# Spreading a factor by one-pass products and adding six tiles to a stored residual by accumulating DMAs

## The reference, cut to what matters

```python
def rmsnorm(x, g):
    y = x * lax.rsqrt(jnp.mean(x * x, axis=-1, keepdims=True) + EPS)
    return y * g

x = x + rmsnorm(merged @ w_o, g_post_mix)
f = jnp.square(jax.nn.relu(rmsnorm(x, g_pre_ffn) @ w1)) @ w2
x = x + rmsnorm(f, g_post_ffn)          # the end: f, its norm per token, the residual
```

## Time and profile before

| | |
|---|---|
| Median of 3 runs | 1711.32 us (1710.51, 1711.32, 1711.40) |
| The profiled execution | 1711.26 us, span 1709.5 us |
| Granted TensorE clock, mean | 0.997 |
| Busy share of the span | TensorE 99%, VectorE 77%, ScalarE 51%, GpSimd 6% |
| From HBM, to HBM | 221.20 MB, 60.69 MB |

### The profile page before, as it was taken

The page is one execution under the profiler, slowest core; times in us unless marked ns, Lnnn a source line. Parts: engine busy times, 40 slices in busy tenths (PEclk is TensorE's granted clock), DMA queues, the critical chain, the costliest instruction groups (busy, mean ns, idle before and its releaser), DMA issues.

```text
span 1709.5 us, 31894 instructions
## 1 busy us (share of the span) xinstructions
PE 1698.6 (99%) x12687; PEld 1685.4 (99%) x12687; DVE 1324.2 (77%) x2538; ACT 868.9 (51%) x1681; POOL 106.2 (6%) x143
## 2 busy tenths in 40 slices
PE   9999999999999999999999999999999999999997
PEld 9999999999999999999999999999999999999997
DVE  7778877878788777668688788777878887777665
ACT  7636454555554545446366374545545536444452
POOL 1311211000000000000002221000000000000000
PEclk9999999999999999999999999999999999999998
DMA  7889989454321322233138898444623313322231
GB/s 249 219 199 215 252 222 241 125 175 155 112 74 51 112 87 87 87 99 99 62 121 221 209 232 217 133 140 114 201 106 99 99 54 98 97 88 87 74 99 56
DMA packets 94133, 233.64 MB, mean 137 GB/s; under 512 B 9888, under 2 KB 21408, under 8 KB 93984
## 3 DMA queue, kind: packets, MB, share of 16 engines
q1 hardware_dynamic: 72352, 179.16, 32.9%
q0 software_dynamic: 20352, 50.34, 14.6%
q10 hardware_dynamic: 1280, 2.10, 0.3%
HBM read 221.20 MB, written 60.69 MB: 165 GB/s over the span
## 4 chain that ended last, share of the span: by engine, by line
PE 99%; DVE 1%; ACT 0%; issue 0%; DVEq 0%
PE ring L820 20%; PE ring L822 20%; PE ring L821 20%; PE att L820 12%; PE att L822 11%; PE att L821 11%; PE att L3680 1%; PE att L815 1%; PE att L814 1%; PE att L827 0%; PE ring L3516 0%; PE att L3496 0%; PE att L828 0%; PE att L3843 0%; ACT rope_s L1289 0%; PE att L3503 0%
## 5 line engine op out<-in xcount | busy, mean ns | idle before, releaser
L820 PE MATMUL ring<-xs_hi,w_lo 128*128 128x288 f32 x1792 | 532.8, 297 | 0.6 <-issue 0.4
L822 PE MATMUL ring<-xs_hi,w_hi 128*128 128x288 f32 x1792 | 527.9, 295 | 0.0
L821 PE MATMUL ring<-xs_lo,w_hi 128*128 128x288 f32 x1792 | 527.7, 294 | 0.0
L2133 DVE TENSOR_TENSOR w_lo<-w_raw,w_hi 128x1024 fp32r<-128x1024 f32 (+1 forms) x370 | 377.1, 1038 | 27.7 <-ACT w_hi L1218 19.0
L820 PEld LDWEIGHTS ring<-xs_hi,w_lo 128*128 128x128 f32 x1792 | 336.6, 188 | 2.9 <-issue 1.2
L821 PEld LDWEIGHTS ring<-xs_lo,w_hi 128*128 128x128 f32 x1792 | 336.8, 188 | 1.3
L822 PEld LDWEIGHTS ring<-xs_hi,w_hi 128*128 128x128 f32 x1792 | 336.6, 188 | 0.0
L822 PE MATMUL att<-f_hi,w_hi 128*128 128x288 f32 x960 | 283.2, 295 | 0.0
L821 PE MATMUL att<-f_lo,w_hi 128*128 128x288 f32 x960 | 282.9, 295 | 0.0
L820 PE MATMUL att<-f_hi,w_lo 128*128 128x288 f32 x960 | 282.6, 294 | 0.0
L820 PEld LDWEIGHTS att<-f_hi,w_lo 128*128 128x128 f32 x960 | 180.4, 188 | 0.0
(11 more groups left out here) (355 smaller groups left out, 3215.5 us busy)
## 6 DMA issues: line engine op xcount, KB each, us to landing
w_raw<-blocks_in SPq DMA_DIRECT2D x189, 512.0 KB, 3.7
weight_sums<-blocks_in POOLq DMA_DIRECT2D x72, 512.0 KB, 7.0
w_raw<-weight_sums SPq DMA_DIRECT2D x96, 256.0 KB, 4.4
w_raw<-blocks_in SPq DMA_DIRECT2D x70, 256.0 KB, 4.2
weight_sums<-weight_sums POOLq DMA_DIRECT2D x48, 256.0 KB, 6.7
small_raw<-small_in SPq DMA_DIRECT2D x16, 320.0 KB, 5.0
small_raw<-small_in SPq DMA_DIRECT2D x32, 128.0 KB, 5.2
my_kept<-rx SPq DMA_DIRECT2D x12, 288.0 KB, 6.1
```

Source lines behind the costliest of these rows:

```text
L820: pe.matmul(out, w[1], x[0], start=first, stop=False)
L821: pe.matmul(out, w[0], x[1], start=False, stop=False)
L822: return pe.matmul(out, w[0], x[0], start=False, stop=last)
L2133: return dve.tensor_tensor(out, a, hi.bitcast(F32), ALU.subtract)
```

## The change

The spread factor is no longer made by three fp32 products but by six fp32r products, from a rounded part `last_hi` and its rest `last_lo`, which VectorE makes after the reciprocal; ScalarE makes a rounded copy of the identity in `last_ident`, ahead of the first `last_scaled`. The tail's pieces are now tiles 0 and 1, 2 and 3, 4 and 5 (`TAIL_SUMMED`) and 6 and 7 (`TAIL_ADDED`). SP stores tiles 0 to 5 of the second half of `x` as they are before the feed-forward result is added, behind its last weight load; GpSimd's queue, once this store has landed, adds each factored piece of `last` straight from SBUF to the stored values in memory. VectorE adds tiles 6 and 7 as before, and ScalarE's queue stores them. SP's last wait is for both kinds.

```diff
-TAIL_MOVED, TAIL_ADDED = [(0, 1), (1, 3), (3, 4)], [(4, 6), (6, 8)]
+TAIL_SUMMED, TAIL_ADDED = [(0, 2), (2, 4), (4, 6)], [(6, 8)]
+SUMMED = TAIL_SUMMED[-1][1]
...
+        sp.wait_ge(pl.x_new, x_new(DEPTH - 1, "wo_b", KC - 1))
+        sp.dma_start(x_out[:, 0:SUMMED, cols(1)], pl.x[:, 0:SUMMED, cols(1)]).then_inc(pl.tail_stored, 16)
         sp.wait_ge(pl.x_new, x_new(DEPTH - 1, "post_a", KC - 1))
         sp.dma_start(x_out[:, :, cols(0)], pl.x[:, :, cols(0)]).then_inc(pl.x_stored, 16)
-        for i, (m0, m1) in enumerate(TAIL_MOVED):
-            sp.wait_ge(pl.tail_moved, i + 1)
-            sp.dma_start(x_out[:, m0:m1, cols(1)], pl.x[:, m0:m1, cols(1)]).then_inc(pl.x_stored, 16)
-        sp.wait_ge(pl.x_stored, 16 * (1 + len(TAIL_MOVED) + len(TAIL_ADDED)))
+        sp.wait_ge(pl.x_stored, 16 * (1 + len(TAIL_ADDED)))
+        sp.wait_ge(pl.tail_summed, 16 * len(TAIL_SUMMED))
...
-        for i, (m0, m1) in enumerate(TAIL_MOVED):
+        pool.wait_ge(pl.tail_stored, 16)
+        for i, (m0, m1) in enumerate(TAIL_SUMMED):
             pool.wait_ge(pl.tail_factored, i + 1)
-            nc.gpsimd.tensor_tensor(pl.x[:, m0:m1, cols(1)], pl.x[:, m0:m1, cols(1)], pl.last[:, m0:m1, :], ALU.add) \
-                .then_inc(pl.tail_moved, 1)
+            pool.dma_start(x_out[:, m0:m1, cols(1)], pl.last[:, m0:m1, :], accum_op=ALU.add).then_inc(pl.tail_summed, 16)
...
+                act.activation(pl.last_ident[0:TRI, 0:TRI], pl.const(C_ID, P)[0:TRI, 0:TRI], ACT.Copy) \
+                    .then_inc(pl.tail_scaled, 1)
                 last_scaled(0)
...
-        dve.reciprocal(pl.last_root[0:TRI, 0:3], pl.last_root[0:TRI, 0:3]).then_inc(pl.tail_spread, 1)
+        own.step(dve.reciprocal(pl.last_inv[0:TRI, 0:3], pl.last_root[0:TRI, 0:3]))
+        own.wait()
+        own.step(dve.tensor_copy(pl.last_hi[0:TRI, 0:3], pl.last_inv[0:TRI, 0:3]))
+        own.wait()
+        minus(pl.last_lo[0:TRI, 0:3], pl.last_inv[0:TRI, 0:3], pl.last_hi[0:TRI, 0:3]).then_inc(pl.tail_spread, 1)
         eng.wait_ge(pl.tail_full, 1)
-        eng.wait_ge(pl.tail_scaled, KC)
-        for m0, m1 in TAIL_MOVED + TAIL_ADDED:
+        eng.wait_ge(pl.tail_scaled, KC + 1)
+        for m0, m1 in TAIL_SUMMED + TAIL_ADDED:
...
         eng.wait_ge(pl.tail_spread, 1)
+        eng.wait_ge(pl.tail_scaled, 1)
         for i in range(3):
-            root_i = pl.last_root[0:TRI, i:i + 1].broadcast_to([TRI, P])
-            last = pe.matmul(att[:, LAST_R + TRI * i:LAST_R + TRI * (i + 1)], root_i, ident[0:TRI, 0:TRI],
-                             start=True, stop=True)
+            out = att[:, LAST_R + TRI * i:LAST_R + TRI * (i + 1)]
+            pe.matmul(out, pl.last_lo[0:TRI, i:i + 1].broadcast_to([TRI, P]), pl.last_ident[0:TRI, 0:TRI],
+                      start=True, stop=False)
+            last = pe.matmul(out, pl.last_hi[0:TRI, i:i + 1].broadcast_to([TRI, P]), pl.last_ident[0:TRI, 0:TRI],
+                             start=False, stop=True)
         last.then_inc(pl.tail_full, 1)
```

More of the change, by code:

```diff
@@ L494, in __init__ @@
         self.tail_added = semaphore("tail_added")
-        self.tail_moved = semaphore("tail_moved")
+        self.tail_stored = semaphore("tail_stored")
+        self.tail_summed = semaphore("tail_summed")
         self.ff_read = semaphore("ff_read")
@@ L575, in memory @@
         self.last_root = self.nc.alloc_sbuf_tensor_at("last_root", [P, 4], F32, offset=self.xh_at + 4 * KC * NH)
+        self.last_inv = self.nc.alloc_sbuf_tensor_at("last_inv", [P, 4], F32, offset=self.xh_at + 4 * KC * NH + 32)
+        self.last_hi = self.nc.alloc_sbuf_tensor_at("last_inv_hi", [P, 4], F32R,
+                                                    offset=self.xh_at + 4 * KC * NH + 64)
+        self.last_lo = self.nc.alloc_sbuf_tensor_at("last_inv_lo", [P, 4], F32R,
+                                                    offset=self.xh_at + 4 * KC * NH + 96)
+        self.last_ident = self.nc.alloc_sbuf_tensor_at("last_ident", [P, P], F32R,
+                                                       offset=self.xh_at + 4 * KC * NH + 128)
         small_at = mark[0]
@@ L855, in program @@
         loads(nc, block, pl, x_in, consts, tables, blocks, small, uv, cache_t, cache_n, cache_pe, x_out)
-        rotation_and_sums(nc, block, pl, blocks)
+        rotation_and_sums(nc, block, pl, blocks, x_out)
         scalar_engine(nc, block, pl, x_in, x_out, kv_out, kpe_out, conv_out)
@@ L1104, in _, with rotation_and_sums @@
             w2_load(7, 3)
+        sp.wait_ge(pl.x_new, x_new(DEPTH - 1, "wo_b", KC - 1))
+        sp.dma_start(x_out[:, 0:SUMMED, cols(1)], pl.x[:, 0:SUMMED, cols(1)]).then_inc(pl.tail_stored, 16)
         sp.wait_ge(pl.x_new, x_new(DEPTH - 1, "post_a", KC - 1))
         sp.dma_start(x_out[:, :, cols(0)], pl.x[:, :, cols(0)]).then_inc(pl.x_stored, 16)
-        for i, (m0, m1) in enumerate(TAIL_MOVED):
-            sp.wait_ge(pl.tail_moved, i + 1)
-            sp.dma_start(x_out[:, m0:m1, cols(1)], pl.x[:, m0:m1, cols(1)]).then_inc(pl.x_stored, 16)
-        sp.wait_ge(pl.x_stored, 16 * (1 + len(TAIL_MOVED) + len(TAIL_ADDED)))
-def rotation_and_sums(nc, block, pl, blocks):
+        sp.wait_ge(pl.x_stored, 16 * (1 + len(TAIL_ADDED)))
+        sp.wait_ge(pl.tail_summed, 16 * len(TAIL_SUMMED))
+def rotation_and_sums(nc, block, pl, blocks, x_out):
     @block.gpsimd
@@ L3451, in _ @@
         for i, (m0, m1) in enumerate(TAIL_ADDED):
-            eng.wait_ge(pl.tail_factored, len(TAIL_MOVED) + 1 + i)
+            eng.wait_ge(pl.tail_factored, len(TAIL_SUMMED) + 1 + i)
             dve.tensor_tensor(pl.x[:, m0:m1, cols(1)], pl.x[:, m0:m1, cols(1)], pl.last[:, m0:m1, :], ALU.add) \
```

## The result

| | time, us (median) | runs | lowest to highest |
|---|---|---|---|
| before, same chip | 1710.38 | 6 | 1709.68 to 1711.40 |
| changed kernel | 1720.32 | 6 | 1719.30 to 1721.29 |

The ratio is 1.0057, with a 95% interval of 1.0047 to 1.0068: 9.9 us slower, where 2.6 were forecast and the range ended at 1717.4. The profiled execution took 1719.3 us, with a span of 1717.5 against 1709.5.

The account below looks back on a forecast made before the run. TensorE bounds all but the tail, whose end passes from VectorE's last add to GpSimd's queue: last landing 1709.1 to 1711.7, span 1712.1, plus 1.76 gives 1713.9 us, 2.6 slower; range 1710.6 to 1717.4.

Parts of the forecast that it names:

- Step 1: VectorE after the reciprocal: a rounding copy and a subtraction, delaying TensorE's first load by 0.39 us.
- Step 2: TensorE's spread: six fp32r products at half clock take 1.57 us against 1.45; first multiply starts 0.52 later.
- lower bound: TensorE's spread takes 0.9 us if the clock holds at 1.00 throughout.
- Steps 3 to 6: Tail: identity copy and residual stores cost nothing; multiplies 0.67 apart; last add takes 0.74, its store lands at 1708.4.
- branch that was to gain 0.7: VectorE's add of tiles 6 and 7 and its store: add ends at 1705.98, against 1706.66 before.
- Step 7: Three GpSimd accumulates of tiles 0 to 5, issued 0.95 apart, paced by queue bytes; last landing at 1711.7 us.
- price of one alone: One 288 KB accumulate on GpSimd's queue, with no other, lands after 5.1 us.
- queue price: Each further 288 KB accumulate in GpSimd's queue costs 1.46 us, by bytes.
- half share of the plain store: Store of tiles 6 and 7 beside the accumulates: half of a share bounded by 0 and 0.8 us.
- first issue's lag: GpSimd's first accumulate can start 0.09 us after the multiply's end, at 1703.29.
- Accumulates paid by the run: Rival, chance 0.26: accumulates cost per run, not per byte, 2.6 us each behind one another; 1717.7 us, or 1721.
- Quick accumulates: Rival, chance 0.12: each accumulate lands within 3.2 us, the plain store lands last; 1710.6 us.

Follow-up runs that it names:

- acc_only: The changed kernel with the spread in fp32 products as before, keeping the residual store and three accumulating DMAs; 1719.71 us, ratio to before 1.0055.
- room_1088: The changed kernel with 1088 bytes of DMA descriptor room (dynamic_dma_scratch_size) in place of 1024; 1719.73 us, ratio to before 1.0054.
- one_run: The changed kernel with the output laid out half by half, so each accumulate has half the runs for the same bytes; 1714.39 us, ratio to before 1.0022.
- plain: The changed kernel with GpSimd's three accumulates turned into plain stores, leaving out the residual's addition in six tiles; 1711.12 us, ratio to before 1.0002.
- acc_two: The changed kernel with only tiles 0 and 1 accumulated by GpSimd, tiles 2 to 7 added by VectorE; 1713.06 us, ratio to before 1.0014.

## Why the prediction was wrong, point by point

**Step 1, VectorE's two more operations: right.** Reciprocal, copy and subtraction start at 1699.33, 1699.54 and 1699.74, and the first load 0.62 after the reciprocal's start, where before had 0.22: 0.40 more, 0.39 said.

**Step 2, the spread: wrong in its clock, 0.7 too dear.** I said that all six products would run at half clock and take 1.57. The six loads started 0.11 apart at full clock, and the first multiply followed 0.91 after the first load, the lower bound that I had given. The changed kernel's windows (us, busy time of PE, PEld, DVE, ACT, POOL, then the granted clock):

```profile
1699.90:1700.80 0.90, 0.85 (x6) 0.74 (x6) 0.00 (x0) 0.00 (x0) 0.00 (x0) 1.00 0.00 0
1700.80:1701.80 1.00, 0.02 (x1) 0.00 (x0) 0.94 (x2) 0.00 (x0) 0.00 (x0) 1.00 0.00 0
1701.80:1702.80 1.00, 0.00 (x0) 0.00 (x0) 1.00 (x2) 0.00 (x0) 0.42 (x1) 0.78 0.00 0
1702.80:1703.80 1.00, 0.00 (x0) 0.00 (x0) 0.97 (x3) 0.00 (x0) 0.82 (x1) 0.50 0.00 0
```

The fall from 2.4 to 1.2 GHz came between 1701.8 and 1702.8 (the mean of 0.78 puts it near 1702.4), 1.7 us later than in the earlier trace rows, and I had taken one execution's moment for a fixed one. From reciprocal to first multiply it is 1.53 where before had 1.70. But the split isn't what gained it: acc_only kept the fp32 products, found the same full clock, and took 1.17. At equal clock the split costs 0.35: 0.39 by VectorE's two operations (0.62 against 0.23 from reciprocal to first load), of which the products give back 0.04 (0.91 against 0.95 from first load to first multiply). In room_1088 the same six products ran at half clock, and reciprocal to first multiply took 2.17.

**Steps 3 to 6: right, but for one landing.** GpSimd's wait ahead of its first accumulate was ended by VectorE's multiply (the 628.96 us idle, above), not by the stored residual; the multiplies start 0.67 apart; the add takes 0.76 (0.74 said). Its store landed 3.5 after the issue where I took 2.3, beside the accumulates; it didn't matter, since it was off the path. The branch that was to gain 0.7 lands at T + 7.1, as before's.

**Step 7, the accumulates: this step failed.** "So issues stand at 1703.29, 1704.24, 1705.19": they began 1.5, 6.6 and 11.5 after T. The price of one alone was nearly right (4.7 for a stated 5.1), and so was its order behind the wait; what was wrong was that a second could be queued before the first had landed. Two issues in a row of before were my evidence; they were of 256 runs and 128, of 2 KB each, which fit together, and 256 with 256 doesn't. The queue price was mis-sized too, though the changed kernel never paid it: 1.46 for each further 288 KB, where the second landed 2.9 behind the first in room_1088, and the others 2.8 and 1.9 apart in one_run. The half share of the plain store, 0.4, doesn't show: the accumulate beside it took 4.8, the two alone 4.6 and 4.7. The first issue's lag was also mis-sized: 0.09 after the multiply's end was arithmetic's distance, and a DMA instruction on GpSimd began 0.77 after it (1702.38, the multiply's end being 1701.61), in before's L1128 0.58 after the landing it waited for.

Put together, from T: 0.75 for the multiply, 0.77 for the lag, then three landings of 4.7 and two turn-arounds of 0.35 make 16.3; 16.2 was measured. The forecast had 9.2 (1711.7 less 1702.46). These 7.0 us are the failure; the time missed by 6.4.

**The rivals.** "Accumulates paid by the run" foresaw the time (1717.7 to 1721; the upper figure leaves out the store's 0.8 that the lower one counts) and its sign. That is luck, since its mechanism, a queue interval of 2.6 to 4.7 on the DMA engines, isn't what the trace shows: the engines rest between the transfers. Runs matter after all, though by the room that they take and not by their time: in one_run half the runs moved the same bytes hardly faster (the second landed 2.8 after the first, in room_1088 with twice the runs 2.9), and yet the end came 5.5 us sooner. "Quick accumulates" has its answer in 4.7 for one alone.

## What to carry to other kernels

Read the waits of every queue to which a change hands work, above all those that end in nothing shown: here a GpSimd that idled on "issue" between DMAs was out of descriptor room, and each further transfer cost a full landing, not its bytes. More room isn't free either: the three kernels that had it reached T 2 to 7 us later than the changed kernel, in one profile each. Count runs before handing GpSimd accumulates, and lay the target out in long runs. A DMA that takes over an add at the end of a kernel is paid by its landing, which here was six times as long as the add.

## What the runs showed of the hardware

- GpSimd's DMAs in flight are limited by the descriptor room that the program reserves: 1024 bytes held three accumulates of 128 runs or one of 256, 1088 two of 256 or one of 256 with two of 128 (but only three of 128), 1152 four of 128; three plain stores of 256 runs fit into 1024. The next issue begins 0.26 to 0.36 after a landing. In the tail it was always the landing of the last one outstanding; in before L1140 was released by L1133's while L1137 was still on its way, 22 times out of 22. When room is given back is not settled.
- The Trainium skill, SBUF — State Buffer, section on SBUF's size, counts 16 KiB per partition for this scratch. This kernel reserves 1 KiB, and the measured limits move with that number.
- An accumulate from SBUF of 288 KB in 256 runs, with no other in flight, took 4.5 to 4.9 us from issue to landing, a plain store of the same shape from GpSimd 2.7 (the first of plain's), and from ScalarE 2.3.
- Beside accumulates a plain store of 288 KB landed after 3.5 (after), 3.8 (acc_two, median of three) and 7.1 us (one_run, behind three of them); beside three plain stores after 3.4 (plain).
- GpSimd begins a DMA instruction 0.6 to 0.8 us after what it waits for, an addition 0.09 after.
- The moment at which TensorE's clock falls in an idle tail differs between executions of like kernels: within the spread in before, plain and acc_two, 1.5 us behind its end in after, ahead of its start in room_1088. It moves the tail by up to 0.65 us.
